# A two-FFN and mixer block on 8 cores: the mixer's window starts a third of a job earlier, w_cond comes in long runs, the mixer has more weight slots, and the last block ends tile by tile

## The reference, cut to what matters

```python
mod = silu(c) @ w_cond + b_cond            # w_cond 1024 x 9*1024, f32: 9 vectors v = 0..8
sh1, sc1, gt1, sh2, sc2, gt2, sh3, sc3, gt3 = split(mod, 9)
h = rmsnorm(x, pre0) * (1 + sc1) + sh1
x = x + 0.5 * gt1 * rmsnorm(swiglu(h), post0)            # FFN 1, d_ff 2816
h = rmsnorm(x, pre1) * (1 + sc2) + sh2
x = x + gt2 * rmsnorm(token_mixer(h), post1)             # attention | HGRN2 recurrence
h = rmsnorm(x, pre2) * (1 + sc3) + sh3
x = x + 0.5 * gt3 * rmsnorm(swiglu(h), post2)            # FFN 2
```

## Time and profile before

| | us |
|---|---|
| runs of the kernel before | 2798.18 median (2756.43, 2798.18, 3007.02) |
| profiled execution, device time | 2758.03 |
| span of its slowest core (core 2) | 2757.0 |
| PE busy in the span | 2484.9 |
| granted TensorE clock, mean (1.0 is 2.4 GHz) | 0.967 |

### The profile page before, as it was taken

One profiled execution on the slowest core, in us unless ns is written; L12 is line 12 of the kernel. 1 busy time (PEld: TensorE's weight loads), 2 busy tenths in 40 slices (PEclk: granted clock), 3 DMA queues, 4 the chain that ended last, 5 costly groups with the idle time before them and its releaser, 6 DMA issues.

```text
span 2757.0 us, 38471 instructions; the slowest of 8 cores (2735.8 to 2757.0 us)
## 1 busy us (share of the span) xinstructions
PE 2484.9 (90%) x13314; PEld 1174.8 (43%) x13314; DVE 1394.0 (51%) x2530; ACT 925.7 (34%) x1650; POOL 190.3 (7%) x292
## 2 busy tenths in 40 slices
PE   1899868799798899899999999899999999989996
PEld 1344423344344444344444444444444444444442
DVE  4552345534465375366475456445746644643242
ACT  1311301123254264164264243514525525331210
POOL 0100100001001001001001000100100200000000
PEclk9999988899999999899999999999999999999998
DMA  9785899947768758868738555573573764547463
GB/s 246 179 228 112 218 229 242 251 149 236 169 163 265 201 163 248 213 163 242 213 132 263 190 186 184 197 248 135 198 251 125 237 217 151 202 159 237 150 207 114
DMA packets 149438, 545.51 MB, mean 198 GB/s; under 512 B 16352, under 2 KB 18656, under 8 KB 141280
## 3 DMA queue, kind: packets, MB, share of 16 engines
q1 hardware_dynamic: 143152, 499.54, 55.7%
q0 software_dynamic: 6096, 43.52, 11.4%
HBM read 517.83 MB, written 94.90 MB: 222 GB/s over the span
## 4 chain that ended last, share of the span: by engine, by line
PE 66%; DMA 20%; DVE 4%; issue 4%; ACT 4%; SPq 2%; POOL 0%; DVEq 0%; ACTq 0%; POOLq 0%
PE psum_all L726 16%; PE psum_all L765 16%; PE psum_all L728 16%; DMA stg<-w_cond 7%; DMA mw<-wm_s 5%; PE psum_all L924 4%; PE psum_all L918 4%; DMA xre<-x2s 2%; PE psum_all L1000 2%; PE psum_all L974 2%; DMA xin<-x 2%; SPq L214 2%; DMA xin<-x2s 1%; PE psum_all L976 1%; DMA fw<-wf_s 1%
## 5 line engine op out<-in xcount | busy, mean ns | idle before, releaser
L726 PE MATMUL psum_all<-hF,fw 128*128 128x512 bf16 x2816 | 681.3, 386 | 46.7 <-DVE act L734 36.1
L728 PE MATMUL psum_all<-hF,fw 128*128 128x512 bf16 x2816 | 675.4, 384 | 18.7 <-DVE tg L732 18.7
L765 PE MATMUL psum_all<-fw,act 128*128 128x512 bf16 x2816 | 637.5, 383 | 10.8 <-DVE ob L777 6.0
L731 ACT ACTIVATE tg<-psum_all 128x512 f32<-128x512 f32 x352 | 210.4, 598 | 858.0 <-PE psum_all L726 856.4
L732 DVE SCALAR_TENSOR_TENSOR tg<-tg,psum_all 128x512 f32<-128x512 f32 x352 | 241.5, 686 | 449.1 <-ACT tg L731 448.5
L726 PEld LDWEIGHTS psum_all<-hF,fw 128*128 128x128 bf16 x2816 | 274.6, 99 | 381.6 <-issue 78.0
L728 PEld LDWEIGHTS psum_all<-hF,fw 128*128 128x128 bf16 x2816 | 274.2, 99 | 354.4 <-issue 48.5
L765 PEld LDWEIGHTS psum_all<-fw,act 128*128 128x128 bf16 x2816 | 272.2, 99 | 331.8 <-issue 30.6
L734 DVE SCALAR_TENSOR_TENSOR act<-tg,psum_all 128x512 bf16<-128x512 f32 x352 | 241.3, 685 | 28.0 <-PE psum_all L728 2.0
L688 DVE SCALAR_TENSOR_TENSOR ob<-ob,est,xre 128x1024 f32<-128x1024 f32 x96 | 123.1, 1283 | 120.2 <-DMA xre<-x 47.9
L777 DVE TENSOR_TENSOR ob<-psum_all,G 128x512 f32<-128x512 f32 x128 | 87.4, 687 | 189.9 <-ACT junk L775 188.9
(11 more groups left out here) (136 smaller groups left out, 1810.3 us busy)
## 6 DMA issues: line engine op xcount, KB each, us to landing
fw<-wf_s SPq DMA_DIRECT2D x416, 512.0 KB, 5.0
mw<-wm_s SPq DMA_DIRECT2D x56, 1024.0 KB, 8.2
stg<-w_cond SPq DMA_DIRECT2D x36, 1024.0 KB, 18.7
wf_s<-w_ffn POOLq DMA_DIRECT2D x17, 1024.0 KB, 14.8
xin<-x SPq DMA_DIRECT2D x32, 512.0 KB, 6.1
xre<-x SPq DMA_DIRECT2D x32, 512.0 KB, 6.8
fw<-w_ffn POOLq DMA_DIRECT2D x32, 512.0 KB, 8.4
wf_s<-fw SPq DMA_DIRECT2D x32, 512.0 KB, 7.8
```

Source lines behind the costliest of these rows:

```text
L726: g = K.op(PE, [(lambda kk=kk: P.matmul(bg.f32(), lhsT=w3[:, kk, 0:128], rhs=h[:, kk, :], start=(kk == 0), stop=(kk == 7))) for kk in rang ...
L728: K.op(PE, [(lambda kk=kk: P.matmul(bu.f32(), lhsT=w3[:, kk, 128:256], rhs=h[:, kk, :], start=(kk == 0), stop=(kk == 7))) for kk in range( ...
L731: th = K.op(ACT, lambda: A.activation(out=tg[:], in_=bg.f32(), func=AF.Tanh, scale=0.5), [bg], [tg_tk], 0.60)
L765: K.op(PE, [(lambda f=f, b=b, tt=tt, wt=wt, f0=f0, ac=ac: P.matmul(b.f32(), lhsT=ac[:, f, tt * 128:(tt + 1) * 128], rhs=wt[:, (f - f0) * 5 ...
```

## The change

- **Modulation.** The host stores w_cond as [9, 128, 8, 1024], so that a DMA of 1 MB reads 8 KB in one run for each partition where it read four runs of 2 KB; a DMA now brings two of the eight row groups for all 1024 columns. The planner takes such a load as 2 MB for v from 2 on. v = 2 is released at chunk 6 of job 0; v = 4 and 3 at chunks 16 and 19 of job 0, v = 5, 7, 6, 8 at chunks 2, 6, 10, 14 of job 1, with planned times 36 us apart where it was 24.
- **Mixer window.** It now goes from the start of the out phase of the job before to 4 us ahead of the out phase of its own job; the Ln waits for the last tanh of the job before. The table `jt` counts the mixer's work as 50 us in the gate/up phase and 26 us in the out phase before.
- **Slots.** `mring` has three slots and K one of its own (`kring`). Paid for by one buffer where there were two or more (`Sb`, `k2c`, `kt`; `qt` two for four), `q2`, `junk`, `ra` and `rb` dropped (they use other tiles), and `fring` with five slots after job 1.
- **xre** has two slots. **Start:** the eleven small loads go to ACT's queue, ahead of ACT's first operation, and the first weight cast waits for the fifth w_cond load, not the fourth.
- **Last job.** The mixer's memory is given to 8 weight slots and 4 `xre` slots, all six chunks of the second half are loaded ahead, and that half is computed tile by tile.
- The planner takes 0.45 us for a DMA issue of SP or ACT (0.08 before) and 300 KB/us for SP (280).

```diff
-    wcond_d = din("w_cond", [D, 9 * D])
+    wcond_d = din("w_cond", [9, 128, 8, D])
-        fring = Rot([take("fw", [128, 2048], BF16) + (K.newsem("fw%d" % i),) for i in range(6)])
+        fring = Rot([take("fw", [128, 2048], BF16) + (K.newsem("fw%d" % i),) for i in range(5)])
-        xre_rot = Rot([take("xre", [128, D], F32) + (K.newsem("xre%d" % i),) for i in range(1)])
+        xre_rot = Rot([take("xre", [128, D], F32) + (K.newsem("xre%d" % i),) for i in range(2)])
-            extra = sum(76.0 / len(w) for w in mix_at.values() if j in w)
-            jt.append((t, t + (115.0 * nb + extra) * 0.66, t + 115.0 * nb + extra))
+            fl = 76.0 * nb + sum(50.0 / len(w) for w in mix_at.values() if j in w)
+            ol = 38.0 * nb + sum(26.0 / len(w) for w in mix_at.values() if j + 1 in w)
+            jt.append((t, t + fl, t + fl + ol))
...
         def load(t, tk, src, nb=16384):
-            K.dma(SP, t[:], src, [], [tk], K.newsem("ld"), nb)
+            K.dma(ACT, t[:], src, [], [tk], K.newsem("ld"), nb)
...
-            for hf in range(2):
-                c0 = v * D + hf * 512
-                for kh in range(2):
-                    stg, stg_tk, stg_sem = stg_rot.next()
-                    wc_ops.append(K.dma(SP, stg[:], wc_view[:, kh * 4:kh * 4 + 4, c0:c0 + 512], [], [stg_tk], stg_sem, 1 << 20, after=after))
+            for q in range(4):
+                stg, stg_tk, stg_sem = stg_rot.next()
+                wc_ops.append(K.dma(SP, stg[:], wcond_d[v, :, 2 * q:2 * q + 2, :], [], [stg_tk], stg_sem, (1 << 20) if v < 2 else (2 << 20), after=after))
...
-                          after=[wc_ops[min(3 + c, 7)]] if c < 6 else [])
+                          after=[wc_ops[min(4 + c, 7)]] if c < 6 else [])
...
+                    last = n == 1 and j == len(jobs) - 1
+                    if last:
+                        wts = [chunk(22 + n * 6 + ci, (f1 - f0) * 512, t0) for ci, (f0, f1) in enumerate(OUT_SPLIT)]
+                    for ci, tt in ([(ci, tt) for tt in range(4) for ci in range(6)] if last else
+                                   [(ci, tt) for ci in range(6) for tt in range(4)]):
...
-            K.T = jt[0][0] + 60.0
-            mod_acc(2, [marks[(0, 8)]])
+            K.T = jt[0][0] + 80.0
+            mod_acc(2, [marks[(0, 6)]])
...
-                K.T = jt[1][0] + 5.0 + 24.0 * i
-                after = [marks[(1, 3 * i)]]
+                K.T = jt[1][0] - 50.0 + 36.0 * i
+                after = [marks[(0, 16 + 3 * i)] if i < 2 else marks[(1, 4 * i - 6)]]
...
-        mring = Rot([take("mw", [128, 8, 512], BF16) + (K.newsem("mw%d" % i),) for i in range(2)])
+        mring = Rot([take("mw", [128, 8, 512], BF16) + (K.newsem("mw%d" % i),) for i in range(NM)])
+        kring = Rot([take("mk", [128, 8, 256], BF16) + (K.newsem("mk"),)])
...
-            w0, w1 = jt[js[0]][0], jt[js[-1]][2]
-            gate = [marks[("tanh", js[0])]]
+            w0, w1 = jt[js[0] - 1][1], jt[js[-1]][1] - 4.0
+            gate = [marks[("tanh", js[0] - 1)]]
...
+            if j == len(jobs) - 1:
+                ss[0] = shared_end
+                fring_e.append(Rot([tmp("fw", [128, 2048], BF16) + (K.newsem("fwe%d" % i),) for i in range(8)]))
+                xre_rot.items = [tmp("xre", [128, D], F32) + (K.newsem("xree%d" % i),) for i in range(4)]
```

137 lines of the change are left out of this document (70 added, 67 removed).

## The result

The changed kernel takes 2602.1 us in its fastest run. On the same chip, run against run, its time is 0.944 of that of the kernel before (95% interval 0.935 to 0.954). Some runs of either kernel have one die at a lower clock (up to 2749 us for the changed kernel, 3007 for the one before); all times and ratios here leave them out, and the other four of the changed kernel lie between 2602.1 and 2622.5. The profiled execution has 2601.0 us on its slowest core, 156 less than the 2757.0 before.

A forecast was written before the change was run, and what follows sets the result against it. TensorE work was taken as the bound, busy 2484.9 of 2757 us, with some 340 us lost to idling and low clock. 2758 - 13 - 5 - 50 - 41 + 12 + 16 - 10 - 16 = 2651, given as 2655; range 2585 to 2735.

The forecast's parts named there:

- The start: Until the first gate/up matmul: small loads leave SP's queue, so w_cond lands earlier; -13 us, from -5 to -17.
- The layout: w_cond loads in 8 KB runs: no gain taken for the longer runs.
- rival 4: w_cond's new layout loads slower, start gives 2 us, job 1 keeps 15 more: 2677; chance 0.20 shared with another rival.
- Job 0: First job: more slack for v = 2, but 8.4 MB more loaded near its end; -5 us, between -10 and +5.
- Job 1: Second job's gate/up phase: w_cond loads stop holding DVE, and so PE; -50 us, between -15 and -62.
- Rival 2: Second job stays bound by DMA, only 15 us come back: 2690 to 2700; chance 0.20 shared with another rival.
- Slots: Mixers: PE's 32.3 us of waits for Q/K weights go, plus slow matmuls after them; -41 us.
- The moved window: Mixers' recurrence moved beside gate/up: +12 us (-25 to +60), +16 for Ln, -10 at output groups.
- Ln group: Mixers: two table loads and four activations on ACT, up to 3 us for each mixer; +16 us, from 0.
- The end: Behind the last matmul: 9 to 10 us left where there were 25; -16 us.
- Rival 1: DVE becomes the mixers' bound and the kernel slower: 2779 to 2814; chance 0.12 half way, 0.05 in full.
- Rival 3: All weights come in time and the planner's order holds DVE: 2597; chance 0.13.

The follow-up runs named there:

- old release: Changed kernel with the w_cond loads' release points, 24 us spacing and 1 MB planner price put back as before; 2654.8 us lowest, ratio 0.964.
- reordered start: Changed kernel with the DVE and ACT operations on gnb, lbl and sinks moved behind the sums of the first eight w_cond loads; 2591.6 us lowest, ratio 0.941.
- old slots: Changed kernel with mixer weights in two slots again, K in the same two, and a semaphore for each second-FFN cast; 2703.2 and 2708.6 us.

## Why the prediction was right, and where it wasn't

The direction and the time were right, and the time in part by luck. The profiled execution gained 156 us where the sum had 107. Of the 49 us between them, 88 were gained in the mixers beyond the forecast, and 38 were missed at the start, in job 0 and in job 1. The four runs of 2602.1 to 2622.5 us lie in the wide range of 2585 to 2735; two of them lie below the 2615 to 2690 that had half the chance.

**The start** (-13, measured +4). The step that failed is "Moving the small loads to ACT delays ACT's first operation by about eleven issues ... so that costs nothing". Its customer on ACT was looked at, and not the ones in DVE's list: `lbt` and `esink` stand ahead of the sums there. With these out of the way the first gate/up matmul is at 60.6 or 59.6, beside the 57 to 60 forecast, so that much of the term was sized rightly. But the start does not end there: "What follows ... keeps its length" failed too. The first tanh comes 5.6 us earlier than before in the best of these runs and not 11, since ACT's list has a tile of x ahead of it (8.2 us of waiting).

**The layout** was rightly taken at nothing, and rival 4 is out. The row of before has 271 GB/s, the same stretch with the new layout and a free list 290, with the old layout 298 and 277. The Trainium skill (DMA: Bandwidth & Descriptors, section on latency and other measured facts) warns of large powers of two in a row's pitch. At the 32 KiB here no such loss shows, since 290 lies between 298 and 277, and none in the time. The 207 GB/s that the prediction took from there is for copies from HBM to HBM, and the same line gives 214 as the full rate, reached with a padded pitch. So 207 is a loss of 3% there, and 51 us in place of 39 does not follow from it. What no rival had is that long packets hold up small loads on another queue.

**Job 0** (-5, measured +1.6): within its bounds. **Job 1** (-50, measured -35): the mechanism was right, as the old release shows, but two of its signs were not. Landing was to fall under 20 us and rose to 29.8: what helped is the distance from release to use, not a shorter queue. And 26 us of waits for L736 and L734 stayed, where under 15 were forecast, from 45 before (the "some 50" took in waits for L732 outside job 1). So the term was 15 us too large; how much of that is these waits was not measured. Rival 2 said 15 us would come back; 35 did, with the casts left in place, and spreading them gave 6 to 10 in another kernel.

**Slots** (-41). In the mixers PE waits 13 us for loads now and waited 54 before: 41 less, where the term had 32 of waiting and 9 of clock. Put back with the old window the slots are worth 54 us (44 and 10), with the new one 85.

**The moved window** (+12, +16, -10, together +18; measured -57 with the slots in place). This is the failed step that matters, and it failed on both sides. The new place: "I take 5 us for each mixer, 40", and 16 for the Ln group, 56 in all. But PE waits only 16 us for DVE and ACT in jobs 2 to 11, where 30 to 50 for DVE alone were forecast. The old place: "Before, it was 30 us of PE work beside 37 and the evictions, so DVE was ahead of PE in neither". I counted DVE's work on both sides, took the one as free and priced only what is new. But the old place had cost 59 us of such waits in the kernel before, beside the evictions of an out phase, and the clock that fell with them; I credited 35, those at L1091, the 8.9 us of the same kind and ten of catT. Of the 88 us by which the mixers beat the forecast, 40 are of the new place, 25 of the old one, 9 of the waits for loads, and the other 14 are PE's busy time at a lower clock, down 27 where some 12 were in the sum. These are sums over the waits of the two profiled executions.

**The end** (-16, measured -15.9), right in all its parts: 10.7 us behind the last matmul, two tiles finished 9.5 us ahead.

**Rival 1** did not come, and is nearer than the result shows. Its cap of 79% was wrong: DVE reaches 42.9 of 50 us in the changed kernel with PE at 50.0.

```profile
1750.00:1800.00 50.00, 50.00 (x340) 24.69 (x339) 42.88 (x98) 23.13 (x41) 2.03 (x2) 1.00 0.53 166
```

But of a further 2.7 us a head, 44 us in jobs 2 to 5, 39 or 61 come through there, so in those jobs the change has little DVE time to spare; in jobs 6 to 11 17 or 18 do. **Rival 3**, at 2597, gave the nearest time, and half of its reasons: the weights came in time and the order does not hold DVE in the mixers, but at the start it does. Its time too is a sum of errors that cancel: start -17, job 0 -8, job 1 -60 and mixers -60, where +4, +2, -35 and -111 were measured.

## What to carry to other kernels

When work moves to another phase, price the waits that it leaves behind as closely as those that it meets; here 59 us were left behind and 16 met, and 35 and 56 had been priced. When loads change queues, look for their readers on every in-order engine, and issue small ones ahead of the bulk, or put their readers behind the bulk's. Read a length to the first instruction that the next phase needs: with the reordered start the matmul came 11 us earlier than before and the tanh behind it only 6. Two edits that feed the same stretch are worth measuring in all four combinations: window and slots gave 110 us together, and the window with the old slots lost 21 in jobs 2 to 5. And where one execution shows something odd, look at its other cores before explaining it by the edit.

## What the runs showed of the hardware

A small load on ACT's queue beside a queued bulk load on SP's takes 20.9 us (`lbl`, 4 KB) and 26.7 (`sinks`) with the bulk in runs of 8 KB, 10.3 and 11.6 with runs of 2 KB; with the reordered start it was 20.0 and 30.4 against 9.4 and 12.0. Issued ahead of the bulk on SP's own queue, as the kernel before does, they took 2.8 and 2.7.

DVE was busy 86% of a 50 us stretch without holding PE up (42.9 us, changed kernel). In another kernel it was busy 88% and PE waited 9.4 us for it, at k2T and kt; whether by its load or by the longer chain is not parted.

The granted clock stood at 0.81 on cores 0 and 1 of one execution (old slots) from 140 to 200 us, with PE busy throughout, where the other six cores of the same execution had 1.00. That is neither of the two levels of 1.2 and 2.4 GHz (0.5 and 1.0), and does not look like a mean of them: from 130 to 250 us every stretch of 20 us on core 1 shows 0.81. It cost core 1 some 20 us, an estimate from job 0 (284 us there, 260 to 267 on the other six cores). Core 1 and core 2 in the same window:

```profile
140.00:200.00 60.00, 60.00 (x226) 24.92 (x225) 33.70 (x50) 11.64 (x17) 3.69 (x7) 0.81 0.90 226
```

```profile
140.00:200.00 60.00, 60.00 (x276) 27.17 (x275) 35.11 (x53) 12.04 (x19) 4.22 (x8) 1.00 1.03 254
```

Its cause stays open.
